# Second projection of layer 1 in three passes on split operands, and the sums of four channel blocks side by side

## What is computed

```python
def conformer_conv_mixer(h, hist, w1, b1, conv_w, conv_b, ln_g, ln_b, w2, b2):
    ag = jnp.einsum("btd,de->bte", h, w1) + b1
    a, g = jnp.split(ag, 2, axis=-1)
    full = jnp.concatenate([hist.astype(h.dtype), a * jax.nn.sigmoid(g)], axis=1)
    c = causal_dwconv(full, conv_w) + conv_b          # 31 taps per channel
    c = jax.nn.silu(layer_norm(c, ln_g, ln_b))        # mean and variance over the channels
    y = jnp.einsum("btc,cd->btd", c, w2) + b2         # the second projection
    return y, full[:, -(CF_WIDTH - 1):]
...
h = layer_norm(ALPHA * h + m, ln1_g[i], ln1_b[i])
f = hierarchical_moe(h, ...)                          # top-1 of 4 groups, top-2 of 8 experts
h = layer_norm(ALPHA * h + f, ln2_g[i], ln2_b[i])
```

## Time and profile before

| | us |
|---|---|
| Median of 3 runs (lowest, highest) | 1183.25 (1183.0, 1187.09) |
| Profiled execution, its own time | 1185.49 |
| Its span in the profile | 1183.7 |
| PE busy in the span | 1030.8 |
| DVE busy | 621.4 |
| ACT busy | 339.4 |
| POOL busy | 241.4 |

### The profile page before, as it was taken

How to read it: one execution, slowest core, us unless ns; L and a number is a source line. 1 busy time by engine, 2 the same in 40 slices (tenths; PEclk the granted TensorE clock), 3 DMA queues, 4 the chain that set the end, 5 groups by cost and what they waited for, 6 DMA issues and landing times.

```text
span 1183.7 us, 16731 instructions
## 1 busy us (share of the span) xinstructions
PE 1030.8 (87%) x5431; PEld 609.4 (51%) x5431; DVE 621.4 (52%) x1105; ACT 339.4 (29%) x492; POOL 241.4 (20%) x374
## 2 busy tenths in 40 slices
PE   6999998992999778888999999999829997799997
PEld 5999996861333223334577777745413332333342
DVE  2322326557444443442729999763474444445536
ACT  3222125112333332332321122340123333334420
POOL 5333334001122111112320132000001221122230
PEclk9999999995999899899999999999959998899999
DMA  8452102049999999985812433500599999999945
GB/s 282 134 174 72 71 1 109 36 171 374 399 406 418 400 389 403 402 326 202 298 40 73 135 117 90 168 13 36 193 353 396 410 405 389 397 392 365 362 165 207
DMA packets 74781, 289.23 MB, mean 244 GB/s; under 512 B 15435, under 2 KB 33983, under 8 KB 48959
## 3 DMA queue, kind: packets, MB, share of 16 engines
q1 hardware_dynamic: 58312, 242.63, 53.2%
q0 software_dynamic: 12320, 26.51, 6.8%
q10 hardware_dynamic: 4103, 19.47, 4.5%
HBM read 279.01 MB, written 28.63 MB: 260 GB/s over the span
## 4 chain that ended last, share of the span: by engine, by line
PE 56%; DVE 17%; DMA 17%; issue 3%; SPq 3%; ACT 2%; POOL 1%; ACTq 0%; DVEq 0%; POOLq 0%
PE ps L1345 15%; PE ps L1148 13%; DMA ring<-in_moe_w_down_dram 8%; PE ps L1360 8%; PE ps L1196 5%; DMA ring<-in_moe_w_up_dram 5%; DVE arena L1934 4%; DVE ring L1934 4%; PE ps L1180 4%; PE ps L1273 3%; PE ps L1331 2%; PE ps L1164 2%; PE ps L1222 1%; DMA arena<-x_rows_dram,now 1%; DVE arena L1807 1%
## 5 line engine op out<-in xcount | busy, mean ns | idle before, releaser
L1345 PE MATMUL ps<-arena 128*64 128x512 f32 x1152 | 275.4, 634 | 38.8 <-DVE arena L1791 36.6
L1345 PEld LDWEIGHTS ps<-arena 128*64 128x64 f32 x1152 | 87.7, 146 | 221.9 <-issue 160.4
L1790 DVE COPY arena<-ring 128x1024 f32 x144 | 99.1, 688 | 110.6 <-SPq L590 67.0
L1360 PE MATMUL ps<-arena 128*64 128x512 f32 x576 | 131.5, 598 | 21.2 <-DVE arena L1807 21.2
L1164 PE MATMUL ps<-arena,ring 128*128 128x296 f32 x512 | 130.4, 417 | 2.4 <-SPq L529 1.6
L1148 PE MATMUL ps<-hT_hi,w_hi 128*128 128x296 f32 x384 | 116.1, 302 | 8.4 <-PE ps L1148 6.8
L1164 PEld LDWEIGHTS ps<-arena,ring 128*128 128x128 f32 x512 | 97.9, 192 | 33.5 <-issue 3.1
L710 ACT COPY arena<-ring 128x1024 f32 x72 | 75.1, 1043 | 138.3 <-SPq L590 57.6
L1148 PE MATMUL ps<-hT_hi,w_lo 128*128 128x296 f32 x384 | 114.5, 298 | 0.0
L1148 PE MATMUL ps<-hT_lo,w_hi 128*128 128x296 f32 x384 | 114.4, 298 | 0.0
L1791 DVE COPY arena<-ring 128x1024 f32 x144 | 98.7, 686 | 0.0
(11 more groups left out here) (271 smaller groups left out, 1319.8 us busy)
## 6 DMA issues: line engine op xcount, KB each, us to landing
ring<-in_moe_w_gate_dram SPq DMA_DIRECT2D x64, 1024.0 KB, 7.9
ring<-in_moe_w_up_dram SPq DMA_DIRECT2D x64, 1024.0 KB, 10.3
ring<-in_moe_w_down_dram SPq DMA_DIRECT2D x64, 1024.0 KB, 10.6
ring<-in_sc_w_in_dram SPq DMA_DIRECT2D x12, 1024.0 KB, 12.3
ring<-y_rows_dram ACTq DMA_DIRECT2D x6, 1024.0 KB, 7.0
ring<-in_cf_w_pw_dram SPq DMA_DIRECT2D x4, 1536.0 KB, 15.6
ring<-in_sc_w_out_dram SPq DMA_DIRECT2D x2, 2048.0 KB, 8.5
x_rows_dram<-ring ACTq DMA_DIRECT2D x8, 512.0 KB, 2.6
```

Of the source, the lines that this page charges most:

```text
L1345: ins = nc.tensor.matmul(ps[own, B_GU, :], xT_e[:, k, own], w_gu[:, x, c, i * 2 * F:(i + 1) * 2 * F], start=(k == 0), stop=(k == C - 1))
L1360: ins = nc.tensor.matmul(ps[own, B_Y + half, :], hidT[:, k, own], w_dn[:, x, k, half * DH:(half + 1) * DH], start=(k == 0), stop=(k == FK ...
L1790: nc.vector.tensor_copy(as_gu(w_gu[:, 0, c, :]), gu_chunk(ranks[0], c))
```

## The change

The second projection of layer 1 takes the form that layer 0 has: the split form replaces `project` for both layers. For it, in layer 1:

- ACT casts the eight blocks of the first half of the weights (five behind square 6 in its order, three behind the last square), and the five tiles of the mix: tile 0 behind the first piece, tile 1 behind the second, tiles 2 to 4 behind the third.
- DVE casts the eight blocks of the second half of the weights, between the last read of a tap result and the mean, and subtracts the rounded part of the mix: tile 0 within the second piece, tile 1 within the third, the others in the tail, as in layer 0.
- POOL makes the rest of all sixteen weight blocks, behind its last `lay_rows`.

The sums of blocks 3, 0, 1 and 2 are made side by side: each block is multiplied with 32 columns of ones into one quarter of the 128 rows of a bank pair of their own (4 and 5). ACT copies the four partial sums, divided by 32 (every sum stands in 32 rows), to `part_sums`, and one block of matmuls with all ones adds them up into the sum. This is done once for the values, ahead of the second group of taps, and once for the squares, behind it. The two added blocks, and values and squares of blocks 4 and 5, now stand between the second and the third group; blocks 6 and 7 stay behind the third. The scratch rows in DRAM get a pitch of 1024 elements instead of 862.

```diff
-        conv_dram = nc.dram_tensor("conv_rows_dram", (3, P, LB), F32).ap()
+        conv_dram = nc.dram_tensor("conv_rows_dram", (3, P, D), F32).ap()[:, :, 0:LB]
...
-        EARLY_SQUARES = 5
+        IN_QUARTERS, B_PARTS = SUMMED[:4], 4
...
+                def copy_parts(i):
+
+                    act.wait_ge(parts_made, i + 1)
+                    if i:
+                        act.wait_ge(value_parts_read, 1)
+                    nc.scalar.activation(part_sums.rearrange("p (a n) -> p a n", a=2), ps[:, B_PARTS:B_PARTS + 2, 0:HALF],
+                                         ACT.Copy, scale=1.0 / QUARTER).then_inc(parts_copied, 1)
+
                 act.wait_ge(g_done, 2 * C)
-                for n in range(EARLY_SQUARES):
+                for n in range(len(IN_QUARTERS)):
                     square(n)
+                copy_parts(0)
+                square(4)
                 read_pe_conv(1)
-                for n in range(EARLY_SQUARES, C):
+                copy_parts(1)
+                for n in range(5, C - 1):
                     square(n)
+                split_out_hi(0, range(5), 1)
+                square(C - 1)
+                split_out_hi(0, range(5, C), 1)
...
                 mix_piece(0)
+                act.wait_ge(b_mixed, C)
+                split_mix_hi(0)
                 state_rows(1, SB)
...
                 mix_piece(1)
+                act.wait_ge(b_mixed, 2 * C)
+                split_mix_hi(1)
                 mix_piece(2)
+                act.wait_ge(b_mixed, 3 * C)
+                for t in range(2, NT):
+                    split_mix_hi(t)
...
                     lay_rows(2)
+                    for half in range(2):
+                        raw = out_raw(half, 1)[1]
+                        for j in range(C):
+                            if half == 0:
+                                pool.wait_ge(out_hi_ready, 2 * C + j + 1)
+                            else:
+                                pool.wait_ge(late_hi_ready, j + 1)
+                            nc.gpsimd.tensor_tensor(out_lo[half][:, j, :], raw[:, j, :], out_hi[half][j][:].bitcast(F32),
+                                                    ALU.subtract).then_inc(out_lo_ready[half], 1)
...
-            def project_split(t, half, js):
+            def project(layer, t, half, js):
...
-                pe.wait_ge(mix_lo_ready, t + 2)
+                pe.wait_ge(mix_lo_ready, layer * NT + t + 2)
                 for j in js:
                     if t == 0:
-                        pe.wait_ge(out_lo_ready[half], j + 1)
+                        pe.wait_ge(out_lo_ready[half], layer * C + j + 1)
...
-                if layer == 1:
-                    pe.wait_ge(b_mixed, C * sum(own.start < t * P + n for _, own in NORM_PIECES))
-                for j in js:
-                    last = nc.tensor.matmul(ps[0:n, 2 * (t % 2) + half, :], mixT[:, j, t * P:t * P + n],
-                                            w[:, j, :], start=(j == 0), stop=(j == C - 1))
...
+            def sum_in_quarters(sources):
+                for a, own in enumerate(halves_of):
+                    for g, src in enumerate(sources):
+                        rows = slice(g * QUARTER, (g + 1) * QUARTER)
+                        last = nc.tensor.matmul(ps[rows, B_PARTS + a, 0:HALF], ones[:, rows], src[:, own], start=True, stop=True)
+                last.then_inc(parts_made, 1)
...
-            pe.wait_ge(glu_done, C - 1)
-            for j in order[:EARLY_SQUARES]:
-                sum_values(j)
+            for j in IN_QUARTERS:
+                wait_values(j)
+            pe.wait_ge(sig_done, C)
+            sum_in_quarters([mixT[:, j, :] for j in IN_QUARTERS])
             conv_taps(1)
+            pe.wait_ge(squared, len(IN_QUARTERS))
+            pe.wait_ge(parts_copied, 1)
+            sum_in_quarters([squares[j] for j in IN_QUARTERS])
             pe.wait_ge(glu_done, C)
-            for j in order[:EARLY_SQUARES]:
-                sum_squares(j)
+            sum_block(B_SUM, part_sums, first=True).then_inc(value_parts_read, 1)
+            sum_values(4)
+            pe.wait_ge(parts_copied, 2)
+            sum_block(B_VAR, part_sums, first=True)
+            sum_squares(4)
+            sum_values(5)
+            sum_squares(5)
             conv_taps(2)
-            for j in (5, 6, 7):
+            for j in (6, 7):
                 sums, squared_sums = sum_values(j), sum_squares(j)
...
             dve.wait_ge(pe_conv_read, 2)
+            n, raw = out_raw(1, 1)
+            dve.wait_ge(weights_ready, n + 1)
+            for j in range(C):
+                nc.vector.tensor_copy(out_hi[1][j][:], raw[:, j, :]).then_inc(late_hi_ready, 1)
...
                     nc.vector.tensor_tensor(mixT[:, j, own], mixT[:, j, own], mean_sb[:, own], ALU.subtract).then_inc(centred, 1)
+                if i == 2:
+                    split_mix_lo(1, layer=1)
                 dve.wait_ge(csd_ready, a + 1)
                 step(nc.vector.reciprocal(rstd_sb[:, own], rstd_sb[:, own]))
+                if i == 1:
+                    split_mix_lo(0, layer=1)
```

## The result

The changed kernel takes 1189.84 us (median of 20 runs) against 1186.68 for the kernel before, measured in turn with it. The ratio is 1.0039, 95% interval 1.0023 to 1.0054: 3 to 6 us slower, where the forecast was 1 us faster. (One run of the twenty was far off, at 2129 us; the ratio leaves it out.) The profiled execution took 1191.85 us, span 1190.1.

A forecast was written before the change was run, and what follows sets the result against it. From the projection's second tile on TensorE was taken to bound, ahead of it VectorE and a transfer. First tile +9.2, four later tiles -10.2: -1.0 us, so 1182.3 from a median of 1183.25; range 1174.5 to 1191.

The forecast's parts named there:

- The projection: Layer 1's second projection: three passes take 13.80 us from tile to tile instead of 16.36; four tiles give 10.2 us.
- Sums and clock: Around the second taps: idle TensorE lowers the granted clock, costing 2.0 us; sums before the third taps take 1.0 + 6.2.
- Casts, SP's wait and splits: Ahead of the first tile: eight VectorE casts 2.75 us, starting 1.42 behind the third taps; two splits 1.2 each.
- GpSimd's subtractions: Sixteen beside VectorE before the first tile: GpSimd stands still while VectorE is dense; VectorE loses 2.8 us, bounds 0 and 12.
- the 8.24: Earlier trace: us one GpSimd product of 1024 columns took beside VectorE's dense taps; read as GpSimd being held out.
- The 1.20: Earlier trace: us a 36-column VectorE instruction took during a GpSimd subtraction; read as VectorE waiting after a gap.
- The late last subtraction: GpSimd's last subtraction, held out by VectorE, ends at 794.9 us; the first tile ends 1.4 us later for it.
- The clock in the first tile: TensorE idles before the projection's first tile and its clock may fall again: 0 to 3 us, taken as 1.2.
- Rival 2: GpSimd takes turns with VectorE before the first tile: twelve subtractions cost 1.0 us each; +6.8 us, 1190.1; chance 0.21.
- Rival 1: Before the first tile the covers hold: no clock fall, no collision of GpSimd and VectorE; -8.4 us, 1174.9; chance 0.27.
- Rival 3: Projection or sums: three passes aren't cheaper, or quarters run one after another; the 10.2 is missing, 1192.5 us; chance 0.04.
- The pitch of the rows in DRAM: Transfer of rows for the third taps: 4,096-byte spacing changes its 9.65 us by -1 to +1, taken as 0.

## Why the prediction was wrong

- **The projection** was right: 13.80 from tile to tile, and from the first tile's end, 797.98 + 2.80 = 800.78, to the end of the projection 54.95 us, where before had 852.82 - 787.56 = 65.26: 10.3 instead of the forecast 10.2.
- **Sums and clock** were right. TensorE stood idle for 3.74 us, the granted clock was 0.50 (1.2 GHz) in the first part of the second taps, 1.8 us by the run that kept it up, where 2.0 was forecast. Between second and third taps 1.00 + 6.27 us, forecast 1.0 + 6.2.
- **Casts, SP's wait and splits** were right: 2.77 for eight casts undisturbed (2.75), 1.23 a split (1.2), the casts 1.4 us behind the third taps. All of it together is seen without the subtractions: mean at +9.6 against the +10.1 forecast, and the addition at +33.4 where the sum without collisions has 787.2, +33.5.
- **GpSimd's subtractions** are the step that failed. The 2.8 us "at four places" measured 10.5. The price of a turn was a little low (0.7 in the sum; 10.5 us for the eleven subtractions from 760.75 on are about 1.0 each); the number of turns was far too low. It came from one row, the 8.24 of the earlier trace rows, read as "GpSimd stands still while VectorE has work without a gap". The six extra subtractions showed what that row is: the time up to the first instruction of VectorE that lets GpSimd in. Afterwards GpSimd got every second turn without any gap of VectorE, and the rows of before behind the 8.24 say the same. At the casts it came 0.8 us after VectorE had begun (760.75 against 759.98) and got in all the same. The 1.20 that pointed the other way was right; it was taken for a price paid only at a gap.
- **The late last subtraction** (794.9) was wrong for the same reason, the other way round: it ended at 775.6, and the last weights never bound the first tile: the 1.4 for it was nothing.
- **The clock in the first tile** was put at 1.2 and cost nothing in the changed kernel: behind the addition it was 1.00 (2.4 GHz), and the first stretch took 8.39 us like the later ones. In the run without the subtractions TensorE stood idle for 2.05 us at the addition, the clock fell to 0.50 (1.2 GHz), and the stretch took 9.91. With these terms the account closes: the first tile's end moved from +33.8 to +48.1, by 14.3, which is the forecast 9.2 plus 7.7 for the subtractions, less 1.4 and 1.2.
- **Rival 2** had the mechanism and nearly the size: twelve turns at 1.0, addition at 799.2 (+45.5), +6.8 us. Measured were 10.5 instead of 12 (five subtractions, not four, fell into the wait for the third taps), and +4.0 at the end of the projection. Its turning point, slower once VectorE loses more than 5.2, is what decided. **Rival 1** shows in the run without the subtractions, as far as collisions go: -5.2 at the end of the projection, not its -8.4, since the clock did fall (1.8 in the second taps, 1.5 in the first tile). **Rival 3** fell with the 13.80.
- **The pitch of the rows in DRAM** wasn't tried by itself. The last of the third group's transfers took 8.8 to 10.4 us in the runs with the new pitch, 9.7 before, so no difference shows, and in no run with the new pitch did the third taps wait for it.

Left open: why VectorE's run of taps held GpSimd out at first, and its run of eight casts did not. The taps read two inputs in SBUF and the casts one, but no run changed that alone. Nor is it shown what lets GpSimd in at the end of a run of taps: once it was the gate, with an input in PSUM, and in the run with the projection alone the closing addition, which has two inputs in SBUF and starts 0.03 us behind the end of the last tap, where the taps themselves overlap.

## What to carry to other kernels

Work that is given to GpSimd "because it is idle" must be priced by what VectorE does meanwhile: here a subtraction that fell between two of VectorE's instructions cost VectorE about 1.0 us (1.1 at a cast), more than the 0.61 for which VectorE does the subtraction itself. Before moving work there, look for VectorE's own waits in the chain (4.18 us for the third taps and 2.4 for the sums here) and for the latest moment at which each piece is needed. And when one row of a trace contradicts another on who waits for whom, as the 8.24 and the 1.20 did, look at what let the waiting one in, and at the rows right behind it, before making a rule of it.

## What was not expected of the hardware

- A GpSimd instruction beside VectorE's dense taps was held out for 7.03 us, with the taps unchanged at 0.83; the same engines a few microseconds later took turns at 1.2 and 1.33.
- In turns VectorE pays far more than its own share: eight casts that take 2.77 us alone took 8.15, and 10.70 and 11.24 where GpSimd had no break, while a subtraction went from 1.26 at the least to a median of 1.39 (by line, in ns):

```profile
L1133 POOL TENSOR_TENSOR out_lo<-ring,out_hi x16: 1262/1387/2084, 751.7 to 774.3; 128x512 fp32r<-128x512 f32 x16
```
